# A divided second product in twelve blocks of PEER's U stage, and norm2's turned input 64 bytes further on

## The reference

```python
def peer_ffn(h, w_q, sub_k1, sub_k2, expert_u, expert_v):
    ht = h.reshape(T, Dm)
    q = (ht @ w_q).reshape(T, PEER_HEADS, PEER_QDIM)
    ...
    experts = jnp.take_along_axis(cand_idx, pos, axis=-1)
    gates = jax.nn.softmax(vals, axis=-1)
    def per_chunk(args):
        xc, ec, gc = args
        u = expert_u[ec]
        a = jnp.einsum('cd,chkd->chk', xc, u).astype(jnp.float32)
        w = (jax.nn.gelu(a) * gc).astype(xc.dtype)
        return jnp.einsum('chk,chkd->cd', w, expert_v[ec])
```

## Time and profile before

| | |
|---|---|
| median of 3 runs | 1714.33 us |
| the profiled execution | 1714.29 us |
| its span on the core | 1712.5 us |
| TensorE, weight loads | 1699.6 us (99%), 1544.7 us (90%) |
| VectorE, ScalarE, GpSimd | 1236.9, 919.6, 383.0 us |
| granted TensorE clock | full speed in nearly all of the span |
| DMA | 346.54 MB, mean 202 GB/s |

### The profile page before, as it was taken

One profiled execution on the slowest core, in us unless ns is written; L12 is line 12 of the kernel. 1 busy time (PEld: TensorE's weight loads), 2 busy tenths in 40 slices (PEclk: granted clock), 3 DMA queues, 4 the chain that ended last, 5 costly groups with the idle time before them and its releaser, 6 DMA issues.

```text
span 1712.5 us, 31053 instructions
## 1 busy us (share of the span) xinstructions
PE 1699.6 (99%) x11336; PEld 1544.7 (90%) x11336; DVE 1236.9 (72%) x2436; ACT 919.6 (54%) x1449; POOL 383.0 (22%) x172
## 2 busy tenths in 40 slices
PE   9999999999999999999999999999999999999998
PEld 8897999899999999988888888877899988889997
DVE  6748749875555555488888887876789966769974
ACT  6568654554545555533333334576476645566653
POOL 1130077437777777500000000000000000000000
PEclk9999999999999999999999999999999999999999
DMA  8561665577777777777777797635545564445562
GB/s 307 197 238 36 193 197 171 199 218 211 206 210 207 212 205 211 226 246 242 238 241 243 266 328 235 231 131 172 198 167 196 197 204 149 164 147 184 190 208 72
DMA packets 120453, 346.54 MB, mean 202 GB/s; under 512 B 13328, under 2 KB 45200, under 8 KB 118928
## 3 DMA queue, kind: packets, MB, share of 16 engines
q1 hardware_dynamic: 118480, 336.70, 61.5%
q10 hardware_dynamic: 1856, 8.23, 1.3%
HBM read 321.03 MB, written 23.86 MB: 201 GB/s over the span
## 4 chain that ended last, share of the span: by engine, by line
PE 95%; ACT 2%; DVE 1%; issue 0%; DMA 0%; POOL 0%; ACTq 0%; DVEq 0%
PE banks L875 60%; PE bank L875 33%; PE bank L1279 1%; ACT wsplit L1680 0%; DVE wsplit L2147 0%; ACT probs L1832 0%; ACT H L1714 0%; PE banks L1279 0%; DMA X<-x 0%; PE bank L930 0%; ACT H L1720 0%; PE bank L1141 0%; PE banks L1092 0%; POOL wsplit L1657 0%; PE bank L942 0%
## 5 line engine op out<-in xcount | busy, mean ns | idle before, releaser
L875 PE MATMUL banks<-HT,wsplit 128*128 128x256 f32 (+1 forms) x3532 | 432.1, 284 | 1.3 <-POOL wsplit L1657 0.6
L875 PEld LDWEIGHTS banks<-HT,wsplit 128*128 128x128 f32 x3532 | 421.0, 189 | 10.3 <-issue 3.4
L1967 ACT ACTIVATE wsplit<-raw 128x1024 fp32r<-128x1024 f32 x252 | 266.4, 1058 | 212.2 <-PE banks L875 201.2
L875 PE MATMUL banks<-wsplit,wexp 128*128 128x512 f32 x1536 | 348.3, 389 | 0.0
L875 PEld LDWEIGHTS banks<-wsplit,wexp 128*128 128x128 f32 x1536 | 288.3, 188 | 59.7
L875 PE MATMUL bank<-HT,wsplit 128*128 128x256 f32 x2688 | 333.2, 283 | 0.0
L875 PEld LDWEIGHTS bank<-HT,wsplit 128*128 128x128 f32 x2688 | 327.2, 192 | 0.0
L1657 POOL TENSOR_TENSOR wsplit<-raw,wsplit 128x1024 fp32r<-128x1024 f32 x114 | 275.4, 2416 | 131.1 <-ACT wsplit L1967 131.1
L1680 ACT ACTIVATE wsplit<-raw 128x1024 fp32r<-128x1024 f32 x146 | 154.3, 1059 | 96.7 <-PE bank L875 48.1
L2147 DVE TENSOR_TENSOR wsplit<-raw,wsplit 128x1024 fp32r<-128x1024 f32 x124 | 151.6, 1235 | 67.3 <-ACT wsplit L1680 66.1
L2730 DVE TENSOR_TENSOR wsplit<-raw,wsplit 128x1024 fp32r<-128x1024 f32 x128 | 156.1, 1219 | 6.2 <-ACT wsplit L1967 6.2
(11 more groups left out here) (333 smaller groups left out, 2022.6 us busy)
## 6 DMA issues: line engine op xcount, KB each, us to landing
raw<-weights SPq DMA_DIRECT2D x148, 512.0 KB, 4.0
raw<-expert_v SPq DMA_DIRECT2D x128, 512.0 KB, 3.6
raw<-expert_u SPq DMA_DIRECT2D x124, 512.0 KB, 3.9
raw1b<-weights SPq DMA_DIRECT2D x102, 512.0 KB, 4.2
raw1a<-weights SPq DMA_DIRECT2D x48, 512.0 KB, 4.5
HT<-acts_parked SPq DMA_DIRECT2D x124, 128.0 KB, 3.4
acts_parked<-act_e SPq DMA_DIRECT2D x62, 128.0 KB, 3.9
acts_parked<-ropeg SPq DMA_DIRECT2D x62, 128.0 KB, 3.8
```

The lines of the kernel that those rows point to most:

```text
L875: ins = pe.matmul(out, lhsT, rhs, start=start, stop=stop, **kw)
L1967: act.activation(wsplit[:, s, 0, :], src, ACT.Copy).then_inc(e_hi, 1)
```

## The change

The turned input of norm2 begins 64 bytes further into its room, like that of the two feed-forward norms, for all who write and read it. And in blocks 0 to 5 of the early blocks and blocks 0 to 5 of the bulk, the product of input chunk 1 is the divided one.

```diff
 DIVIDED = {"ffu": {(0, 1): 24, (1, 0): 24, (1, 1): 24, (2, 0): 24, (2, 1): 24, (3, 0): 24}}
-HT_BEGINS = {"ffn0": 16, "ffn1": 16}
+HT_BEGINS = {"ffn0": 16, "ffn1": 16, "norm2": 16}
...
             turn_second_by_factors("norm2", Hp, X1, open_bank(("pq", 0)), 0)
             pe.wait_ge(in_more, 16)
-            feature_groups(("pq",), ("wq",), range(3), HT, "norm2")
+            feature_groups(("pq",), ("wq",), range(3), HT_at("norm2"), "norm2")
...
-                    feature_groups(("pq",), ("wq",), queries_behind(hp), HT)
+                    feature_groups(("pq",), ("wq",), queries_behind(hp), HT_at("norm2"))
...
                 w = tiles_of(lambda part: wsplit[:, u_slot(n), part, :], k=KD)
                 for k in range(KD):
-                    ins = mm3(b[:, 0:S], lambda a: w(a)[:, k, :], lambda c: HT[:, c, k, :], k == 0, k == KD - 1)
+                    if n < 6 and k == 1:
+                        mm3_divided(b[:, 0:S], lambda a: w(a)[:, k, :], lambda c: HT_at("norm2")[:, c, k, :], 24)
+                        continue
+                    ins = mm3(b[:, 0:S], lambda a: w(a)[:, k, :], lambda c: HT_at("norm2")[:, c, k, :], k == 0, k == KD - 1)
                 ins.then_inc(bank_full, 1)
...
                 w = tiles_of(lambda part: wsplit[:, u_slot(m + EARLY), part, :], k=KD)
                 for k in range(KD):
-                    ins = mm3(PS[m % 2][:, 0:S], lambda a: w(a)[:, k, :], lambda c: HT[:, c, k, :], k == 0, k == KD - 1)
+                    if m < 6 and k == 1:
+                        mm3_divided(PS[m % 2][:, 0:S], lambda a: w(a)[:, k, :], lambda c: HT_at("norm2")[:, c, k, :], 24)
+                        continue
+                    ins = mm3(PS[m % 2][:, 0:S], lambda a: w(a)[:, k, :], lambda c: HT_at("norm2")[:, c, k, :], k == 0, k == KD - 1)
                 ins.then_inc(a_full, 1)
...
-            norm_out("norm2", HT)
+            norm_out("norm2", HT_at("norm2"))
```

## The result

The changed kernel takes 1701.58 us (median of 4 runs, 1701.52 to 1701.89), the kernel before 1714.36 us on the same chip (4 runs): a ratio of 0.9926, 95% interval 0.9915 to 0.9938. It is 12.8 us faster, where 7.5 were forecast; 1701.58 lies inside the range of 1691 to 1713, 5.2 us under the predicted 1706.8, and outside the narrower range of 1704 to 1709 that the forecast itself had. The profiled execution has a span of 1699.6 us against 1712.5, both at a granted clock of 1.00 (0.999 in the mean).

The account below looks back on a forecast made before the run. TensorE's matmul pace was taken as the bound. Savings of 0.67 (queries), 1.80 (early blocks), 0.29 and 4.71 us (bulk) summed to 7.47, giving 1706.8 us from 1714.29; range 1691 to 1713, the forecast's own 1704 to 1709.

Parts of the forecast that it names:

- The reading: Whole kernel: TensorE, busy 99% of the span, is the bound, so the time between matmul starts counts.
- step 1: Query products behind norm2: shifted but undivided, 360 of them go from 120.0 to 118.1 ns, saving 0.67 us.
- steps 2 and 3: Early blocks: 0 and 1 gain nothing, hidden behind GpSimd; 2 to 15 run at 113.33 ns, saving 1.80 us after divisions.
- Step 4: Bulk blocks 0 to 5 of U: fast pace saves 0.96 us, less 0.67 for six divisions, leaving 0.29 us.
- step 5: Bulk blocks 6 to 111 of U: 2544 products at 118.1 ns, saving 4.71 us; bounds zero and 16.97 us.
- step 6: The 256 unshifted gate products in U: stay at 120.0 ns, zero gain; other bound 1.71 us.
- Cover: U: GpSimd, 2.41 us per block and 2.3 us ahead, and DMA under 88% wouldn't stop a faster TensorE.
- A: U: the fast pace survives the gate groups, saving 21.4 us, 1692.9 us in all; chance 0.30.
- B: U: the shift alone is worth nothing and gate groups end the fast pace; 2.1 us saved, 1712.2 us; chance 0.15.
- C: U: changing between gate and U products costs 3.8 us, divisions 1.1; slower at 1719.2 us; chance 0.09.
- D: Bulk U: divisions don't bring the fast pace, so blocks 0 to 5 lose 0.7 us; chance 0.46 shared with the forecast.

Follow-up runs that it names:

- divide_only: The changed kernel with its divided products kept but norm2's turned input back at the start of its room: 1715.71 us, ratio 1.0009 to the kernel before.
- shift_only: The changed kernel with norm2's turned input still 64 bytes further on but no divided product in U: 1701.52 us, ratio 0.9926 to the kernel before.
- weights_shifted: The changed kernel with the whole weight tile moved 64 bytes instead, and every norm's turned input at its room's start: 1708.03 us.
- close_pairs_divided: The changed kernel with gate groups paired three products apart in one block, plus a division straight behind each pair's second group: 1710.04 us.
- gates_shifted: The changed kernel with the gate products' moving operand also shifted, beginning 64 bytes ahead of the weight tile: 1705.64 us.
- gates_in_close_pairs: The changed kernel with gate groups paired three products apart in one block, bulk divisions only in blocks 0 and 1: near 1695.7 or 1706.4 to 1707.0 us.
- gates_in_pairs: The changed kernel with the 64 gate groups in 32 pairs at consecutive blocks, bulk divisions only in blocks 0 and 1: 1697.59 us.

## Why the prediction came out as it did

1. **The reading held.** TensorE's pace was the whole matter: the gain is in the starts of the 256-wide products, at one clock, and V and both up-projections didn't move. That the 64 bytes might do nothing is refuted by divide_only at 120.0, shift_only at 117.8 and 113.3, and weights_shifted at 113.75. The Trainium skill (TensorE: Matmul & The Clock Gate, Part 2, section Step-by-step: what each phase is for) states that TensorE has two independent SBUF read ports and that a weight load takes no read bandwidth from the running matmul. That the bytes' place then does nothing was the prediction's own conclusion: the section doesn't speak of the place of an operand, and no run here looks at the two reads apart, so whether they disturb each other isn't shown.
2. **Queries (step 1):** forecast 0.67 us, measured 0.75. The pace is 117.8 in place of 118.1.
3. **Early blocks (steps 2 and 3):** forecast 1.80, measured 1.76; blocks 0 and 1 are hidden behind GpSimd's low part as reckoned (323.00 to 326.03, block 2 at 326.17). Within the two hidden blocks the first division (at 319.97) left the slow pace and the second one (322.90) ended it. That the divisions brought the fast pace here was luck of place, as close_pairs_divided shows.
4. **The bulk (steps 4 and 5) was the mis-sized term**: forecast 0.29 + 4.71 = 5.0 us, measured 10.9. Step 4 was right in size; step 5 was 4.71 against some 10.7 (10.6 behind the group at 386.76 and 0.16 of block 6, which is fast). The step that failed is "After block 5 there is no division any more. I take 118.1". It took the slow pace as what comes behind unshifted products, from the one row that had it. That row shows a stage that is entered once. In U the products are entered 61 times behind block 6, and every second time the unshifted group leaves them at 113.3: 115.8 in the mean. The bounds of the step, 0 and 16.97 us, held. 10.7 lies near the middle between all slow and all fast, 2544 x (1.85 + 6.67)/2 = 10.8, which is what nearly half of the products at the fast pace must give. The forecast named its own weak place (the pace behind a gate group), but the total fell into the range because the bounds of this step were wide, and not because its pace was known.
5. **Gate products (step 6):** forecast zero, and they stay at 120.1 ns in the mean, by turns 119.3 and 121.0.
6. **Cover:** TensorE waits for nobody between 328 and 706 us; GpSimd still needs 2.41 us a block:

```profile
480.33 2.41 POOL L1663 TENSOR_TENSOR wsplit<-raw,wsplit 128x1024 fp32r<-128x1024 f32 x1 [0.31 <-ACT wsplit L1973]
...
485.28 2.88 PE L875 MATMUL bank<-HT,wsplit 128*128 128x256 f32 x24
```

It ends at 482.74, 2.5 us ahead of the block that reads it. DMA rises from 72% to 76% between 400 and 700 us and from 83% to 86% in the early part, under the 88% reckoned.

7. **The rivals.** A (the fast pace survives everything, 1692.9) is half true of the change, and true of U's products in weights_shifted, which pays for it in V. B and C are refuted: the shift is all there is, and a group takes 0.48 to 0.49 us from either pace, where it took 0.48. D is right in its price, since the divisions gain nothing in the bulk (342.63 us in shift_only against 343.02), and wrong in its cause: in the bulk too the divisions behind the gate groups bring the fast pace (three products from 381.20 start 121, 118 and 118 ns apart, those behind the division at 381.55 settle at 113). They gain nothing because the groups bring it as well.

The sum with what was measured: 0.75 (queries) + 1.76 + 10.92 = 13.43, less 0.11 by which the queries begin later and 0.01 before block 2, is the 13.31 us at the start of V; less 0.46 between V and the up-projection it is 12.85, the 12.9 between the spans.

## What to carry to other kernels

Where TensorE is busy 99% and an equal shape runs at two paces in one trace, divide length by count in the chain of waits for every stage, and then look at both operands' first byte: here 64 bytes were worth 0.75% of the kernel. Before trusting one row for the pace "behind" some other kind of product, ask how often and from which pace it is entered, and try it in both; a pace that depends on what came before isn't a price per product. A tile that is one product's weights and another's moving operand can't be moved for one of them alone.

## What the runs showed of the hardware that I had not expected

- The same 256-wide products at a granted clock of 1.00 have these steady paces: 120.0 ns with both operands at their old places, 117.8 or 113.3 ns with the moving operand 64 or 192 bytes on, and 118.7 or 120.0 with 128. Which of the two holds depends on what ran before, and it stays until something else is issued: 260 early products of the changed kernel in one pace (335.32 to 364.80), through changing banks and weight slots.
- Four unshifted products of another kind turn the pace over in both directions, in three kernels at every group; with other things close by (the close pairs, and divisions straight behind a group) a slow pace can also stay slow. Shifted ones (gates_shifted) only end the fast one. A divided product does either, by what stands ahead of it.
- 512-wide products have two paces as well, 226.7 ns and, with the weight tile 64 bytes on, 233.3. The move that makes the 256-wide ones of U fast makes them slow.
- One program, gates_in_close_pairs, had two times, three runs near 1695.7 and four from 1706.4 to 1707.0 us. What differs between such executions stays open; a wait of 0.5 us left one trace slow and another fast. gates_in_pairs, at 1697.59 us within 0.4 us in its four runs, is the version I would keep.
